# Experts in alternation, the four smallest in 64 slots with high and low token parts side by side

## The reference

```
logits = ht @ w_router + b_router                 # (256, 8)
top_val, top_idx = lax.top_k(logits, 2)
gates = jax.nn.softmax(top_val, axis=-1)
combine = sum(one_hot(top_idx, 8) * gates[..., None], axis=1)
for e in range(8):
    y = y + combine[:, e:e+1] * ((silu(ht @ w_gate[e]) * (ht @ w_up[e])) @ w_down[e])
```

## Time and profile before

| | us |
|---|---|
| median of three runs | 1531.63 (1528.27 to 1533.59) |
| the profiled execution, its own time | 1534.6 |
| its span, first to last instruction | 1532.8 |
| TensorE busy | 1453.3 (95%) |
| VectorE busy | 1161.0 (76%) |
| ScalarE busy | 967.3 (63%) |
| HBM read | 420.77 MB |

### The profile page before, as it was taken

How to read it: one execution, slowest core, us unless ns; L and a number is a source line. 1 busy time by engine, 2 the same in 40 slices (tenths; PEclk the granted TensorE clock), 3 DMA queues, 4 the chain that set the end, 5 groups by cost and what they waited for, 6 DMA issues and landing times.

```text
span 1532.8 us, 18738 instructions
## 1 busy us (share of the span) xinstructions
PE 1453.3 (95%) x6705; PEld 1187.3 (77%) x6706; DVE 1161.0 (76%) x1147; ACT 967.3 (63%) x944; POOL 39.0 (3%) x47
## 2 busy tenths in 40 slices
PE   7977999999879699999999999999999999999997
PEld 6764788888757588888888888888888888888885
DVE  4675454552674689799889888889988979988884
ACT  4445444333485567777677687777777777776772
POOL 0003000000022000000000000000000000000000
PEclk9997999999899699999999999999999999999999
DMA  9540555643522199999999999999999999999993
GB/s 321 189 145 1 165 167 163 211 157 93 165 73 72 67 345 370 341 358 368 346 353 366 366 347 356 366 345 356 363 345 359 365 347 355 368 346 354 366 367 118
DMA packets 184055, 422.50 MB, mean 276 GB/s; under 512 B 7889, under 2 KB 14791, under 8 KB 184007
## 3 DMA queue, kind: packets, MB, share of 16 engines
q1 hardware_dynamic: 182908, 419.10, 76.9%
q0 software_dynamic: 864, 2.68, 0.5%
q10 hardware_dynamic: 234, 0.09, 0.0%
HBM read 420.77 MB, written 1.07 MB: 275 GB/s over the span
## 4 chain that ended last, share of the span: by engine, by line
PE 91%; DVE 5%; ACT 2%; issue 1%; ACTq 0%; DMA 0%; POOL 0%; DVEq 0%
PE PS L1207 28%; PE PS L1209 27%; PE PS L1208 27%; PE PS L1545 2%; DVE w_lo L654 1%; PE PS L1503 1%; PE PS L1527 1%; PE PS L1307 1%; PE PS L1528 1%; PE PS L1268 0%; DVE w_lo L1055 0%; ACT w_hi L296 0%; PE PS L1290 0%; PE PS L1289 0%; PE PS L1512 0%
## 5 line engine op out<-in xcount | busy, mean ns | idle before, releaser
L1055 DVE TENSOR_TENSOR w_lo<-raw,w_hi 128x2048 fp32r<-128x2048 f32 x336 | 762.3, 2287 | 121.7 <-ACT w_hi L557 121.7
L557 ACT ACTIVATE w_hi<-raw 128x2048 fp32r<-128x2048 f32 x336 | 622.3, 1907 | 10.1 <-DMA raw<-in_w_up_o_dram 6.8
L1207 PE MATMUL PS<-w_hi,a_hi 128*128 128x512 f32 (+4 forms) x1312 | 513.0, 391 | 16.6 <-DVE w_lo L654 6.5
L1209 PE MATMUL PS<-w_hi,a_lo 128*128 128x512 f32 (+4 forms) x1312 | 505.8, 386 | 0.0
L1208 PE MATMUL PS<-w_lo,a_hi 128*128 128x512 f32 (+4 forms) x1312 | 505.0, 385 | 0.0
L1207 PEld LDWEIGHTS PS<-w_hi,a_hi 128*128 128x128 f32 x1312 | 250.0, 191 | 65.1 <-issue 14.6
L1209 PEld LDWEIGHTS PS<-w_hi,a_lo 128*128 128x128 f32 x1312 | 249.8, 190 | 49.0
L1208 PEld LDWEIGHTS PS<-w_lo,a_hi 128*128 128x128 f32 x1312 | 250.4, 191 | 45.7
L1207 PE MATMUL PS<-w_hi,e_hi 128*128 128x512 f32 x448 | 178.1, 398 | 0.0
L1209 PE MATMUL PS<-w_hi,e_lo 128*128 128x512 f32 x448 | 177.3, 396 | 0.0
L1208 PE MATMUL PS<-w_lo,e_hi 128*128 128x512 f32 x448 | 176.9, 395 | 0.0
(11 more groups left out here) (244 smaller groups left out, 1072.1 us busy)
## 6 DMA issues: line engine op xcount, KB each, us to landing
raw<-in_w_gate_o_dram SPq DMA_DIRECT2D x112, 1024.0 KB, 5.1
raw<-in_w_up_o_dram SPq DMA_DIRECT2D x112, 1024.0 KB, 5.1
raw<-in_w_down_o_dram SPq DMA_DIRECT2D x112, 1024.0 KB, 5.0
raw<-in_w_in_e_dram SPq DMA_DIRECT2D x12, 1024.0 KB, 8.1
raw<-in_w_down_e_dram SPq DMA_DIRECT2D x11, 1024.0 KB, 4.9
raw<-in_w_gate_e_dram SPq DMA_DIRECT2D x10, 1024.0 KB, 5.1
raw<-in_w_up_e_dram SPq DMA_DIRECT2D x10, 1024.0 KB, 5.1
raw<-in_w_out_e_dram SPq DMA_DIRECT2D x4, 1024.0 KB, 5.0
```

The costliest lines, as they stand in the source:

```text
L557: nc.scalar.activation(w_hi[:, c % STG, :], raw[:, c % RAW, :], ACT.Copy).then_inc(hi_done, 1)
L1055: nc.vector.tensor_tensor(w_lo[:, c % RAW, :], raw[:, c % RAW, :], w_hi[:, c % STG, :], ALU.subtract).then_inc(lo_done, 1)
L1207: nc.tensor.matmul(dst, xh, wh, start=first, stop=False)
L1209: return nc.tensor.matmul(dst, xl, wh, start=False, stop=last)
```

## The change

The experts are taken in another order: expert 0 first, and the others ranked by their number of tokens, so that places 0, 2, 4, 6 hold the four of highest rank (`large`) and places 1, 3, 5, 7 the four of lowest (`small`). `by_size` works this out on VectorE; `order` tells SP which expert's weights to load from place 1 on, and `pos` and `comb` are rearranged to match. A `large` place is as before, with 128 slots.

A `small` place has 64 slots (`HALF`). `picks` writes the 64 columns twice, so the gathered block is there twice, and `turned` puts the high part in columns 0 to 63 of `a_hi` and the low part in columns 64 to 127. One pass with the high weights and one with the low weights then multiply both parts: eight matmuls a chunk (`both`), and the low x low product comes in too. ScalarE copies both PSUM tiles out (`sge`, `he`); TensorE's transpose is a matmul with `fold`, two 64 x 64 identities on top of one another, which adds the two halves. Silu and the product with the up tile are done on the transposed form of 256 columns (`sT`, `hT`), and its high and low part go side by side into `e_hi`. More than 64 tokens in a `small` place count as `need`.

The loops run over three pairs, with the last pair written out. Ahead of the stage `turned(0)` stands before the splits of chunks 1 to 3, `gates` and `by_size` behind them, and TensorE waits for `count_set` in place of `need_set`.

```diff
@@ SP
-            with sp.Fori(0, NE) as e:
-                expert_weights(e, e)
+            expert_weights(0, 0)
+            sp.wait_ge(sem("order_set"), 1)
+            with sp.Fori(1, NE) as p:
+                expert_weights(p, sp.value_load(order[0:1, bass.ds(p, 1)], min_val=0, max_val=NE - 1))
...
@@ ScalarE, small
+            def small(i, n, follow):
+
+                for k in range(ELEAD, EXPERT_CHUNKS + ELEAD * follow):
+                    esplit(i, k)
+                    if k % 4 == 1 and 9 <= k <= DOWN + 5:
+                        j = (k - 9) // 4
+                        act.wait_ge(sem("sm_tr"), j + 1 + n * FE_TILES)
+                        if j >= 2:
+                            act.wait_ge(sem("sm_mul"), j - 1 + n * FE_TILES)
+                        nc.scalar.activation(sT[:, j % 2, :], PS[:, 6 + j % 2, 0:4 * HALF], ACT.Silu).then_inc(sem("sm_silu"), 1)
+                    if k % 4 == 1 and 5 <= k <= DOWN + 1:
+                        j = (k - 5) // 4
+                        act.wait_ge(mm_done, C_MOE + 4 * j + 4 + i * EXPERT_CHUNKS)
+                        if j >= 2:
+                            act.wait_ge(sem("sm_tr"), j - 1 + n * FE_TILES)
+                        nc.scalar.activation(sge[:, j % 2, :], PS[:, gate_bank(j), :], ACT.Copy)
+                        nc.scalar.activation(he[:, j % 2, :], PS[:, up_bank(j), :], ACT.Copy).then_inc(sem("sm_ev"), 1)
+                    if k % 4 == 3 and 11 <= k <= DOWN + 7:
+                        j = (k - 11) // 4
+                        act.wait_ge(sem("sm_mul"), j + 1 + n * FE_TILES)
+                        nc.scalar.activation(e_hi[:, 4 * j:4 * j + 4, 0:HALF],
+                                             hT[:, j % 2, :].rearrange("p (f t) -> p f t", f=4), ACT.Copy)\
+                            .then_inc(sem("sm_hi"), 1)
...
@@ VectorE, ahead of the stage
             step(nc.vector.tensor_scalar(R(7), PS[:, 4:6, 0:NE], FAR, None, ALU.add))
             step(nc.vector.tensor_tensor(R(7), R(7), R(6), ALU.mult))
...
-            nc.vector.tensor_scalar(need[:, 0:NE], PS[0:1, 6, 0:NE], -float(P), None, ALU.add)
...
+            step(nc.vector.tensor_scalar(pos[:, :, 0:1], R(7)[:, :, 0:1], -FAR, None, ALU.add))
+
+            def by_size():
...
+                nc.vector.tensor_copy(order[:, :], row(4)[0:1, :]).then_inc(sem("order_set"), 1)
...
@@ VectorE, small
+                    if k % 4 == 2 and 10 <= k <= DOWN + 6:
+                        j = (k - 10) // 4
+                        dve.wait_ge(sem("sm_silu"), j + 1 + n * FE_TILES)
+                        if j >= 2:
+                            dve.wait_ge(sem("sm_hi"), j - 1 + n * FE_TILES)
+                        nc.vector.tensor_tensor(hT[:, j % 2, :], PS[:, 6 + j % 2, 4 * HALF:8 * HALF], sT[:, j % 2, :], ALU.mult)\
+                            .then_inc(sem("sm_mul"), 1)
+                    if k % 4 == 0 and 12 <= k <= DOWN + 8:
+                        j = (k - 12) // 4
+                        dve.wait_ge(sem("sm_hi"), j + 1 + n * FE_TILES)
+                        nc.vector.tensor_tensor(e_hi[:, 4 * j:4 * j + 4, HALF:P],
+                                                hT[:, j % 2, :].rearrange("p (f t) -> p f t", f=4),
+                                                e_hi[:, 4 * j:4 * j + 4, 0:HALF], ALU.subtract).then_inc(sem("sm_lo"), 1)
...
@@ VectorE, the start of the stage
-            picks(0, 0)
+            picks(0, P)
+            nc.vector.tensor_copy(row(0), PS[:, 6, 0:NE]).then_inc(sem("count_set"), 1)
             esplit(0, 0)
-            gates()
-            gated_picks(0, 0)
+            turned(0, P)
             for k in range(1, ELEAD):
                 esplit(0, k)
-            turned(0)
-            with dve.Fori(0, NE - 1) as e:
-                expert(e, True)
-            expert(NE - 1, False)
+            gates()
+            by_size()
+            gated_picks(0, 0, P)
+            with dve.Fori(0, PAIRS - 1) as n:
+                large(2 * n, n, True)
+                small(2 * n + 1, n, True)
+            large(NE - 2, PAIRS - 1, True)
+            small(NE - 1, PAIRS - 1, False)
...
@@ TensorE
-            pe.wait_ge(sem("need_set"), 1)
...
+            def turn_small(i, n, j):
+                pe.wait_ge(sem("sm_ev"), j + 1 + n * FE_TILES)
+                if j >= 2:
+                    pe.wait_ge(sem("sm_mul"), j - 1 + n * FE_TILES)
+                else:
+                    pe.wait_ge(sem("moe_add"), 4 * i + j + 1)
+                for u, halves in enumerate((sge, he)):
+                    for f in range(4):
+                        at = (4 * u + f) * HALF
+                        ins = nc.tensor.matmul(PS[:, 6 + j % 2, at:at + HALF], halves[:, j % 2, f * P:(f + 1) * P], fold[:, :],
+                                               start=True, stop=True)
+                ins.then_inc(sem("sm_tr"), 1)
...
+            def both(dst, xs, wh, wl, first, last):
+                nc.tensor.matmul(dst, xs, wh, start=first, stop=False)
+                return nc.tensor.matmul(dst, xs, wl, start=False, stop=last)
```

More of the change, by code:

```diff
@@ L201, in hybrid_trunk @@
         xg, z = place(z, "xg", [P, D])
+        sT, z = place(z, "sT", [P, 2, 4 * HALF])
+        fold, z = place(z, "fold", [P, HALF])
+        hT, _ = place(zr + FFE, "hT", [P, 2, 4 * HALF])
         y_lo, z = place(0, "y_lo", [P, D], f32r)
@@ L577, in result, with large @@
                                      scale=st[:, 90:91]).then_inc(sem("moe_yhi"), 1)
-            def expert(i, follow):
+            def large(i, n, follow):
                 for k in range(ELEAD, EXPERT_CHUNKS + ELEAD * follow):
@@ L623, in _ @@
                         gathered(i)
-                        turned(i)
-                        expert(i, False)
+                        turned(i, P)
+                        large(i, e + PAIRS, False)
                     with act.Else():
@@ L1092, in add_back, with back, large @@
                                             PS[:, BACK[s], :], ALU.add).then_inc(sem("moe_add"), 1)
-            def expert(i, follow, alone=False):
+            def back(i):
+                dve.wait_ge(sem("moe_turn"), i + 1)
+                nc.vector.tensor_reduce(st[:, 90:91], PS[:, 4, 0:S], AX.X, ALU.add)
+                nc.vector.tensor_scalar(backT[:, :], PS[:, 4, 0:S], 0.0, None, ALU.is_gt).then_inc(sem("moe_back"), 1)
+            def large(i, n, follow, alone=False):
                 for k in range(ELEAD, EXPERT_CHUNKS + ELEAD * follow):
@@ L1129, in expert, with small @@
                     add_back(i + 1)
-            picks(0, 0)
+            def small(i, n, follow):
+                for k in range(ELEAD, EXPERT_CHUNKS + ELEAD * follow):
+                    esplit(i, k)
+                    if 6 <= k < 10:
+                        add_back(i, [k - 6])
+                    if k % 4 == 2 and 10 <= k <= DOWN + 6:
[11 more added lines that the diff above has]
+                                                e_hi[:, 4 * j:4 * j + 4, 0:HALF], ALU.subtract).then_inc(sem("sm_lo"), 1)
+                    if k == PICK_AT + 4:
+                        back(i)
+                    if follow and k == PICK_AT + 8:
+                        picks(i + 1, P)
+                    if follow and k == PICK_AT + 9:
+                        gated_picks(i + 1, i + 1, P)
+                    if follow and k == GATHER_AT + 7:
+                        turned(i + 1, P)
+                    if follow and k == EXPERT_CHUNKS + ELEAD - 1:
+                        result(i)
+                if not follow:
+                    result(i)
@@ L1546, in turn, with between, large @@
                 ins.then_inc(sem("moe_tr"), 1)
-            def expert(i, follow, alone=False):
+            def turn_small(i, n, j):
[10 more added lines that the diff above has]
+                ins.then_inc(sem("sm_tr"), 1)
+            def between(i, k, follow, alone=False):
+                if k == BRING_AT and not alone:
+                    bring_back(i)
+                if k == PICK_AT:
+                    if not alone:
+                        pe.wait_ge(sem("moe_add"), 4 * i + 4)
+                    turn_pick(i)
+                if follow and k == GATHER_AT:
+                    pe.wait_ge(sem("moe_back"), i + 1)
+                    gather(i + 1)
+                if follow and k == GATHER_AT + 3:
+                    turn_block(i + 1)
+            def large(i, n, follow, alone=False):
                 pe.wait_ge(sem("moe_xlo"), 2 * i + 2)
@@ L1594, in _ @@
             gather(0)
             turn_block(0)
-            with pe.Fori(0, NE - 1) as e:
-                expert(e, True)
-            expert(NE - 1, False)
+            pe.wait_ge(sem("count_set"), 1)
+            with pe.Fori(0, PAIRS - 1) as n:
+                large(2 * n, n, True)
+                small(2 * n + 1, n, True)
+            large(NE - 2, PAIRS - 1, True)
+            small(NE - 1, PAIRS - 1, False)
             bring_back(NE)
@@ L1608, in _ @@
                         turn_block(i)
```

(2 more changed lines are left out.)

172 lines of the change are left out of this document (117 added, 55 removed).

## The result

The changed kernel takes 1478.69 us (median of four runs, 1478.08 to 1482.54) against 1532.61 us of the kernel before: a ratio of 0.9656, 95% interval 0.9627 to 0.9685, 3.4% faster. The forecast was 1480.0, in a range of 1462 to 1508. Its mechanism held, but that it came within 1.3 us is luck, for its misses cancelled: the small experts and the start came out cheaper than forecast, and a stall that it did not have took 13 us back.

What follows compares the result with a forecast made beforehand. TensorE was taken to bound the expert stage at 123.5 us an expert. From the profiled 1534.6, four small experts save 12.5 us each and the start 2, giving 1482.6; the runs' median lies 3.0 lower, so 1480, range 1462 to 1508.

Steps and rivals of the forecast that it cites:

- the start: Start of the expert stage: first expert matmul 4 to 5 us earlier, at about 526; a gain of 2 us counted.
- TensorE stops being the bound in small experts: Small experts: TensorE needs 88 us, at most 105, while VectorE's floor is 104.9 us.
- the chain: Small experts' gate and up: dependent steps through ScalarE, VectorE and TensorE set the pace, giving 111 us an expert.
- The clock rival: Small experts: gaps under a microsecond lower TensorE's clock, an expert takes 118 to 124 us, total 1505 to 1534; chance 0.06.
- A round of 10.3 us: Small experts' gate and up: four chunks take 10.3 us through ScalarE and VectorE; seven rounds are 72.1 us.
- the fold: Small experts' transposes on TensorE: seven times eight matmuls of 64 columns at 0.11 us, 6 us in all, 23 by upper bound.
- the earlier branch: Within a small-expert round: w_lo of chunk 4j+7 and TensorE's eight matmuls end at T+10.0, before the other branch's T+10.3.
- The down half at 35.2 us: Small expert's down half: runs at VectorE's pace, 14 × 2.27 + 3.4 = 35.2 us.
- a ceiling of 384 GB/s: Weight loads: at 384 GB/s a large and small pair needs 229.4 us and gets 234.5, so transfers are narrowly hidden.
- the rival that rested on it: Expert stage: 357 GB/s is the DMA ceiling, a small expert takes 123.4 us, total 1529 to 1534, no gain; chance 0.04.
- The store of the slots: Passage from large to small expert: seven slots carry over some 9 us of loads, 7 at faster pace, covering 3.7 us.
- the 3 us to be given back: First expert: by_size delays w_lo of chunk 4 some 1.5 us, additions to X another 1; net start gain counted 2 us.

Runs made afterwards that it cites:

- e5: Changed kernel with SP's loop written out, odd-place experts loading half of each chunk and fold matmuls one chunk earlier: 1464.63 us, ratio 0.9537 to the kernel before.
- e1: Changed kernel with TensorE's loop over pairs written out, the other engines keeping theirs: 1464.43 us, ratio 0.9528 to the kernel before.
- e4: Changed kernel with experts at odd places loading only half of each chunk and SP's loop written out: 1479.29 us, ratio 0.9639 to the kernel before.
- e7: Changed kernel with the four large experts first, then the four small ones, instead of alternating: 1474.85 us, ratio 0.9614 to the kernel before.
- e6: Kernel before with only the new start: VectorE's turned(0) ahead of the splits of chunks 1 to 3, gates behind them: 1527.91 us, ratio 0.9957.
- e9: Changed kernel with all eight places large, keeping the order by size, SP's register loads and the new start: 1520.24 us, ratio 0.9907 to the kernel before.

## Why the prediction was right, step by step

- **TensorE stops being the bound in small experts; VectorE and the chain take over.** Right: 12.0 us of 112 idle, VectorE 104.09 busy (104.9 forecast) at clock 1.00. ScalarE's 90.4 us (96 forecast) bound nothing. The clock rival did not come: gaps of up to 1.6 us left it at the full level. It came at the jumps instead.
- **A round of 10.3 us, limited by ScalarE and VectorE.** The mechanism was right and the branch wrong: it is 11.05, through TensorE. The mis-sized term is the fold, taken at 0.11 us a matmul from the transposes, the nearest in columns, and measured at 0.21: a plain f32 matmul is two instructions of 0.11 us each, a transpose is one; the upper bound from the row was 0.405. I had looked at its bounds only as TensorE's work, where they cost nothing, and let a turn of 0.9 us pass in the chain as the earlier branch, by 0.3 us. Another 0.8 us made it the later one. Shown by the round above and by e5. The forecast had 72.1 us of rounds and 3.4 of work beside them, 75.5; gate and up took 73.7. Six rounds are 66.5 us; the first four chunks, split ahead, take only 7.5, at TensorE's pace (647.35 to 654.81), and the work beside lies within the rounds.
- **The down half at 35.2 us.** Right: 35.1 in e1 and e4 by TensorE's starts. So a small expert is 108.8 to 108.9 us where 111 was forecast, by two misses of opposite sign in gate and up.
- **The DMA engines hide it, narrowly, with a ceiling of 384 GB/s.** Right, and narrower than narrow: 387 at 2 KB rows, 405 in the down half. By the Trainium skill, "DMA: Bandwidth & Descriptors", section "Bandwidth", a core beside a streaming neighbour is held to about 358 GB/s. A stretch of 112 us at 393 GB/s, in a kernel on one core, does not show that limit; the rival that rested on it fell. The store of the slots is real: e7.
- **The start.** 4.8 us gained (forecast 5 at best). Of the 3 us to be given back 1.2 came, the first expert's 125.0 against 123.8 in e6: a wait for `w_lo` of chunk 4 as forecast (1.29 us in e1, 1.5 forecast), or the low clock in its place. Against the kernel before, whose clock was low there too, the first expert still gains 0.9. SP's loads: no cost seen.
- **Missing: the jump back.** No step of the prediction looked at the code's size. (238.6 − 232.0) = 6.6 us a turn, 13.2 in two: 4.5 of gap and some 2 of matmuls at half clock. e1 measured 12.8.
- **The sum as it should have been:** three small experts at 108.9 instead of 123.5 are 43.8, the last one 13.7 (107.1 against 120.8); the first large one 0.9, the three others at 123.1 another 1.3; less 13.2 for the jumps, plus 4.8 at the start and 0.7 at the end: 52.0, against 51.8 in the profiles.

TensorE's work in a small expert fell from 123.5 us to some 94 (an estimate: 76.8 of matmuls, 12 of folds, some 5 of the rest), by 29, and half of that arrived: 14.6. The rest went to two limits that lay together at 109 us.

Left open: why the down half of a large expert takes 0.5 us less after the change than before (41.8 and 42.4), in e7 and e9 too; its instructions are the same. Why some 4 us are gained ahead of the stage, and why the clock is low behind the first expert matmul in the changed kernel and e9 and full in e1 and e6, with the same wait of 1.5 us before it. And why the gap is 4.5 us in one kernel and 1.8 in the other was argued, not shown.

## What to carry to other kernels

When an engine that bounds a stage is relieved, compute the next limits separately, and then look whether two of them coincide: here one edit alone was worth nothing, the other 1 to 3 us, and the pair 12.6. Price every new instruction twice, as work and as a link of the chain in which it stands. And when a loop body grows, count its instructions: look at the instruction queue's loads in steady state, for a body that is loaded anew on each turn costs a stall where the loop jumps back, and writing the loop out (for that one engine) took it away here: 12.8 us, a better version than the change itself.

## What the runs showed of the hardware that I had not expected

- The instruction queue made one 16 KB load in 740 us with a body of some 1,120 TensorE instructions and 29 with one of some 2,060; a jump back then stopped TensorE for 4.5 us where it had no work queued, and for 1.8 us where it was the bound.
- A plain f32 matmul of 64 moving columns is two instructions in the trace and took 0.21 us, twice the 0.11 us of a transpose of 128 columns.
- The DMA engines held 387 GB/s at a share of 1.05 with 2 KB rows and 405 at 1.02 in the down half, where rows are 4 KB.
- A TensorE that is idle in gaps of up to 1.6 us, about one in every round of 11 us, kept 2.4 GHz through the small experts; one gap of 4.49 us went with 1.2 GHz for the next five (0.63 from 758 to 760 us, 0.50 to 765, 0.94 to 768).
